# Channel-major tensors and row tiles by token residue modulo 16, with only the pooling input in time order

## The reference, cut to what matters

```
u     = rms_norm(x) * g                     # x: (4, 4096, 1024)
proj  = u @ w_in                            # 5120 columns: a, gate, p, two gates
v     = a * sigmoid(gate)                   # GLU
v     = depthwise_causal_conv(v, width 31)  # over time
v     = swish(layer_norm(v)) @ w_conv_out   # conv branch
z     = trailing_mean(p, w) - p             # w = 2, 4, 8, 16, one per group of 256 channels
z     = (z @ pool_w[g]) * pool_scale @ w_pool_out
h     = x + rms_norm((g_conv * v + g_pool * z) @ w_o)
out   = h + rms_norm(square(relu(rms_norm(h) @ w_ff1)) @ w_ff2)
```

## Time and profile before

| | us |
|---|---|
| time, median of 3 runs | 975.74 |
| time, lowest | 975.29 |
| time of the profiled execution | 976.0 |
| span of its slowest core (the spans run from 971.7 to 974.4) | 974.4 |
| busy in that span: PE / DVE / ACT / POOL | 949.2 / 451.3 / 277.6 / 62.6 |

### The profile page before, as it was taken

How to read it: one execution, slowest core, us unless ns; L and a number is a source line. 1 busy time by engine, 2 the same in 40 slices (tenths; PEclk the granted TensorE clock), 3 DMA queues, 4 the chain that set the end, 5 groups by cost and what they waited for, 6 DMA issues and landing times.

```text
span 974.4 us, 14114 instructions; the slowest of 8 cores (971.7 to 974.4 us)
## 1 busy us (share of the span) xinstructions
PE 949.2 (97%) x4971; PEld 484.2 (50%) x4971; DVE 451.3 (46%) x767; ACT 277.6 (28%) x531; POOL 62.6 (6%) x112
## 2 busy tenths in 40 slices
PE   7789999999999999999999999999999999999996
PEld 4655666665545544444444444444444444444444
DVE  4478886575482114566666630344223431244222
ACT  4553111132114431333335530233202330133211
POOL 1010001000010000121213200000000000000000
PEclk9999999999999999999999999999999999999999
DMA  9995165976780021759989995220022001210021
GB/s 183 253 146 74 17 89 105 143 109 115 118 140 1 1 87 15 143 117 191 168 190 178 196 197 90 87 87 1 1 87 87 1 1 44 87 43 1 1 86 66
DMA packets 93111, 91.21 MB, mean 94 GB/s; under 512 B 43601, under 2 KB 74577, under 8 KB 92914
## 3 DMA queue, kind: packets, MB, share of 16 engines
q0 software_dynamic: 32416, 35.13, 26.2%
q1 hardware_dynamic: 60626, 55.18, 21.1%
HBM read 98.88 MB, written 16.84 MB: 119 GB/s over the span
## 4 chain that ended last, share of the span: by engine, by line
PE 91%; DMA 3%; DVE 3%; ACT 1%; issue 1%; DVEq 0%; ACTq 0%; SPq 0%
PE ps L220 90%; DMA arena<-w_in 2%; DMA arena<-xh 1%; ACT arena L238 1%; PE ps L223 1%; DVE arena L246 1%; DVE arena L250 1%; DVE arena L477 0%; DMA arena<-arena 0%; DVE arena L241 0%; ACT sm L238 0%; DVE arena L256 0%; DVEq L159 0%; DVE sm L400 0%; ACTq L159 0%
## 5 line engine op out<-in xcount | busy, mean ns | idle before, releaser
L220 PE MATMUL ps<-arena 128*128 128x512 bf16 (+4 forms) x4731 | 937.9, 360 | 13.9 <-DVE arena L246 2.8
L220 PEld LDWEIGHTS ps<-arena 128*128 128x128 bf16 (+1 forms) x4731 | 470.1, 103 | 473.4 <-issue 25.7
L238 ACT ACTIVATE arena<-ps 128x512 bf16<-128x512 f32 (+5 forms) x346 | 203.0, 593 | 622.1 <-PE ps L220 467.0
L246 DVE TENSOR_SCALAR ps<-ps 128x512 f32<-128x512 f32 x128 | 89.1, 699 | 110.9 <-PE ps L220 110.2
L241 DVE TENSOR_TENSOR ps<-ps,arena 128x512 f32<-128x512 f32 (+1 forms) x65 | 43.6, 688 | 176.1 <-ACT arena L238 175.6
L250 DVE SCALAR_TENSOR_TENSOR arena<-arena,ps 128x512 bf16<-128x512 f32 (+1 forms) x64 | 43.9, 686 | 133.0 <-ACT arena L238 111.0
L241 DVE TENSOR_TENSOR arena<-ps,arena 128x512 bf16<-128x512 f32 (+2 forms) x52 | 42.3, 830 | 35.6 <-ACT arena L238 29.6
L238 ACT ACTIVATE arena<-arena 128x1024 bf16<-128x1024 f32 (+1 forms) x33 | 34.8, 1054 | 46.3 <-DVE arena L250 35.8
L250 DVE SCALAR_TENSOR_TENSOR arena<-ps,sm,arena 128x512 f32<-128x512 f32 (+1 forms) x65 | 45.1, 737 | 5.0 <-DVE sm L400 3.0
L250 DVE SCALAR_TENSOR_TENSOR arena<-arena,sm 128x1024 bf16<-128x1024 f32 (+1 forms) x33 | 42.3, 1282 | 4.3 <-POOL sm L396 2.4
L241 DVE TENSOR_TENSOR arena<-arena 128x512 bf16<-128x512 f32 (+2 forms) x56 | 38.4, 690 | 4.3
(11 more groups left out here) (34 smaller groups left out, 91.3 us busy)
## 6 DMA issues: line engine op xcount, KB each, us to landing
arena<-xh SPq DMA_DIRECT2D x32, 512.0 KB, 8.6
arena<-w_ff POOLq DMA_DIRECT2D x16, 1024.0 KB, 27.8
out<-arena SPq DMA_DIRECT2D x31, 512.0 KB, 3.1
arena<-out SPq DMA_DIRECT2D x16, 512.0 KB, 4.1
arena<-w_in POOLq DMA_DIRECT2D x12, 512.0 KB, 13.1
arena<-w_in POOLq DMA_DIRECT2D x2, 2048.0 KB, 17.2
arena<-gb SPq DMA_DIRECT2D x4, 512.0 KB, 6.4
arena<-w_pool_out POOLq DMA_DIRECT2D x2, 1024.0 KB, 23.1
```

The source lines that it names most:

```text
L220: kb.op("pe", lambda e: e.matmul(o, lhsT=l, rhs=r, start=start, stop=stop), [l, r], [o])
L238: kb.op("act", lambda e: e.activation(out=o, in_=i, func=func, **kw), rd, wr)
L246: kb.op("dve", lambda e: e.tensor_scalar(out=o, in0=a, scalar1=s1, scalar2=s2, op0=op0, **kw), rd, [o])
```

## The change

Columns of `uT`, `z`, `s_t` and all that follows them no longer run in time. Column r*128 + m now holds token 16*m + r. A tile j of x and of the output is the 128 rows j, j+16, j+32, ..., each still 4 KB long, 64 KB apart in DRAM. `p_t` stays in time order, so that the copies from PSUM write it in steps of 16 columns (64 bytes), with the 16 halo columns as a copy of their own, and every pooling task now writes `z` in steps of 128 columns (256 bytes). Since a residue tile spans all of time, a pooling task needs the whole row of its chunk: the tasks are queued only behind block 3 of a chunk. The `p_group`s go in the order 0, 7, 1, 2, 3, 6, 5, 4; one task is emitted behind each of the last eight, two behind each pair of `q` = 0 and one behind each of `q` = 1. The stationary operand of a GLU product becomes 128 neighbouring columns, and the activation of `cv_t3` writes them in one piece (its input view is left as it was).

```diff
--- before.py
+++ after.py
@@ -187,6 +187,8 @@
     gbd = din("gb", [5, DM])
     convw = din("convw", [8, 128, 16 * 3 * 16])
     out = nc.dram_tensor("out", [NT, DM], F32, kind="ExternalOutput").ap()
+    xrows = xh[H:TT, :].rearrange("(m r) d -> r m d", r=16)
+    orows = out.rearrange("(m r) d -> r m d", r=16)
     hud = nc.dram_tensor("hu_scratch", [H, DM], BF16, kind="Internal").ap()
 
     with ExitStack() as es:
@@ -358,8 +360,8 @@
         wev = []
 
         def x_load(j):
-            P, r0 = (32, 0) if j < 0 else (128, H + 128 * j)
-            xev[j] = LOAD(xst[x_buf[x_order.index(j)]][:P], xh[r0:r0 + P, :].rearrange("p (k t) -> p k t", k=8),
+            P, src = (32, xh[0:32, :]) if j < 0 else (128, xrows[j])
+            xev[j] = LOAD(xst[x_buf[x_order.index(j)]][:P], src.rearrange("p (k t) -> p k t", k=8),
                           after=[wev[j - 4]] if j in (4, 5, 6) else [])
 
         LOAD(grow, gbd[0:1, :])
@@ -454,14 +456,16 @@
             w = POOL_W[g]
             c0 = 32 + blk * 512
             pc = p_t[:, cc, :]
-            zo = z[:, cc, blk * 512:(blk + 1) * 512]
+            zo = z[:, cc, :].rearrange("p (r m) -> p m r", r=16)[:, 32 * blk:32 * (blk + 1), :]
+            z0 = z[:, cc, :].rearrange("p (r m) -> p m r", r=16)[:, 0, :]
+            tm = lambda v: v.rearrange("p (m r) -> p m r", r=16)
             if g == 0:
-                TTE("dve", zo, pc[:, c0 - 1:c0 + 511], pc[:, c0:c0 + 512], ALU.subtract)
+                TTE("dve", zo, tm(pc[:, c0 - 1:c0 + 511]), tm(pc[:, c0:c0 + 512]), ALU.subtract)
                 if blk == 0:
                     t1 = scr16
                     TTE("dve", t1, pc[:, 31:47], pc[:, 32:48], ALU.add)
                     TTE("dve", t1, t1, inv[:, 0, :], ALU.mult)
-                    STT(zo[:, 0:16], pc[:, 32:48], -2.0, t1, ALU.mult, ALU.add)
+                    STT(z0, pc[:, 32:48], -2.0, t1, ALU.mult, ALU.add)
                 return
             sb = s2b[2] if g == 1 else s2b[cc % 2]
             if g == 1:
@@ -479,11 +483,11 @@
                 if blk < 3:
                     COPY("dve", carry[:, cc:cc + 1], so[:, n - 1:n])
                 sl = so[:, n - 512:n]
-            STT(zo, sl, 1.0 / w, pc[:, c0:c0 + 512], ALU.mult, ALU.subtract)
+            STT(zo, tm(sl), 1.0 / w, tm(pc[:, c0:c0 + 512]), ALU.mult, ALU.subtract)
             if blk == 0:
                 t1 = scr16
                 TTE("dve", t1, sl[:, 0:16], inv[:, g, :], ALU.mult)
-                TTE("dve", zo[:, 0:16], t1, pc[:, 32:48], ALU.subtract)
+                TTE("dve", z0, t1, pc[:, 32:48], ALU.subtract)
 
         scr = T("scr", [128, 16 + 8], F32)
         scr16 = scr[:, 0:16]
@@ -495,7 +499,12 @@
             b = banks(1)
             for k in range(8):
                 MM(ps[:, b, 0:n], w_p[:, k, cc * 128:(cc + 1) * 128], uT[:, k, H + t0:H + t0 + n], k == 0, k == 7)
-            COPY(eng, p_t[:, cc, 32 + t0:32 + t0 + n], ps[:, b, 0:n])
+            h = max(-t0, 0)
+            if h:
+                COPY(eng, p_t[:, cc, 32 - h:32], ps[:, b, 0:h])
+            r0, r1 = (t0 + h) // 128, (t0 + n) // 128
+            COPY(eng, p_t[:, cc, 32:2080].rearrange("p (m r) -> p r m", r=16)[:, r0:r1, :],
+                 ps[:, b, h:n].rearrange("p (r m) -> p r m", m=128))
 
 
         def wg_load(q):
@@ -532,14 +541,13 @@
             (trn, 7), (pu, 6, 2), (nrm, 9), (pu, 7, 2), (pu, 0, 3), (nrm, 10), (pu, 1, 3), (pu, 2, 3), (nrm, 11),
             (pu, 3, 3), (pu, 4, 3), (nrm, 12), (pu, 5, 3), (nrm, 13), (pu, 6, 3), (nrm, 14), (wg_load, 0), (pu, 7, 3),
             (nrm, 15), (wg_load, 1)])
-        for blk in range(2):
-            for cc in range(8):
-                pq(cc, blk)
         for blk in range(2, 4):
-            for cc in range(8):
+            for cc in pools:
                 pg(cc, blk)
-                pq(cc, blk)
-                pool_pump(1)
+                if blk == 3:
+                    for b in range(4):
+                        pq(cc, b)
+                    pool_pump(1)
 
 
         def conv_load(cc):
@@ -576,7 +584,7 @@
             for i in range(2):
                 r = 2 * rp + i
                 for k in range(8):
-                    MM(ps[:, b + i, :], uT[:, k, H + r:H + NT:16], wg[q % 2][:, k, :, :].rearrange("p a n -> p (a n)"), k == 0, k == 7)
+                    MM(ps[:, b + i, :], uT[:, k, H + r * 128:H + (r + 1) * 128], wg[q % 2][:, k, :, :].rearrange("p a n -> p (a n)"), k == 0, k == 7)
             sg = sig[st["sig"]]
             st["sig"] ^= 1
             sg = sg.rearrange("p (a n) -> p a n", a=2)
@@ -659,7 +667,7 @@
                 glu_pair(q, rp)
                 if steps:
                     steps.popleft()()
-                pool_pump(1)
+                pool_pump(2 if q == 0 else 1)
                 pump(3)
                 if q == 3 and rp % 2 == 0:
                     weff_group(rp // 2)
@@ -709,7 +717,7 @@
             TS(v, v, bnag[:, r, 0:1], ALU.subtract, lnr[:, r:r + 1], ALU.mult)
 
         def cv_t3(cc):
-            sv = s_t[:, cc, :].rearrange("p (m r) -> p m r", r=16)
+            sv = s_t[:, cc, :].rearrange("p (r m) -> p r m", r=16)
             pbs = []
             for half in range(2):
                 b = banks(1)
@@ -718,7 +726,7 @@
                 for r8 in range(8):
                     TR(pb[:, r8 * 128:(r8 + 1) * 128], cv[:, cc, half * 8 + r8, :], identb[:])
             for half in range(2):
-                ACT(sv[:, :, half * 8:half * 8 + 8], pbs[half].rearrange("p (r m) -> p m r", r=8), AF.Silu,
+                ACT(sv[:, half * 8:half * 8 + 8, :], pbs[half].rearrange("p (r m) -> p r m", r=8), AF.Silu,
                     bias=vcol(8, cc), scale=vcol(0, cc))
 
         for blk in range(4):
@@ -752,7 +760,7 @@
         outh = {}
 
         def x_reload(j):
-            LOAD(xr[j % 3], xh[H + 128 * j:H + 128 * (j + 1), :])
+            LOAD(xr[j % 3], xrows[j])
 
         def resid_sq(p, c0, gb_t, junk, ac):
 
@@ -779,7 +787,7 @@
                     if c0 <= c < c0 + n:
                         rs = res[:, c:c + p.shape[1]]
                         STT(rs, p, r, rs, ALU.mult, ALU.add)
-                rs, dst = res[:, c0:c0 + n], out[128 * j:128 * (j + 1), c0:c0 + n]
+                rs, dst = res[:, c0:c0 + n], orows[j][:, c0:c0 + n]
                 outh[j, c0] = kb.op("sp", lambda e, rs=rs, dst=dst: e.dma_start(out=dst, in_=rs), [rs], [("outh", j)], dma=True)
 
         def halves(b):
@@ -865,7 +873,7 @@
 
         def ff2_end(b, j):
             res = xres[j % 2]
-            LOAD(res, out[128 * j:128 * (j + 1), :], reads=[("outh", j)])
+            LOAD(res, orows[j], reads=[("outh", j)])
             resid_b(halves(b), resid_a(b, gb3, 0, hT[j // 4][:, 0, :], "act"), res, j)
 
         def ff2_tile(j):
```

## The result

The changed kernel takes 1031.35 us where the kernel before takes 975.67: 1.06 times as long, 95% interval 1.0507 to 1.0694. The forecast was 985.5 with a range to 1000. Where executions of an experiment were disturbed (two of four of the one called e3, one of four of e2, one of eleven of e7), the others stand for it.

The account below looks back on a forecast made before the run. TensorE, busy 97% of the span, was taken to bound the kernel, with VectorE's queue on its path in the GLU stage. 7.5 + 1.6 + 0.7 = 9.8 us on 976.0, less 0.3, gave 985.5, range 977 to 1000.

Parts of the forecast that it names:

- Steps in writing: Stepped copies into p_t and pooling writes of z: between nothing and 0.53 us for 512 columns on VectorE, taken as nothing.
- The first rival: Stepped writes cost the full 0.53 us, VectorE falls further behind and ScalarE's ramp copies lengthen: 998 us; chance 0.22.
- the ramp: Before the GLU stage, eight more copies of 16 columns on ScalarE: 0.7 us, between 0 and 1.4.
- The moved pooling: Pooling moved from the ramp's end into GLU part 0 makes VectorE late with conv weights, delaying TensorE: 7.5 us.
- the clock: Behind TensorE's wait of some 6 us for conv weights, a lower granted clock costs 1.6 us, bounds 0 and 3.2.
- its wait: In GLU part 1, TensorE waits some 6 us for conv weights, ready at 141.4.
- The weight loads of the GLU: TensorE's loads for GLU products fall from 142 to 98 ns each, and give nothing.
- Loads of x with rows 64 KB apart: Loading tiles of x as 4 KB rows 64 KB apart: taken as 0, bounds 0 and 3 us.

Follow-up runs that it names:

- e3: The changed kernel, but the copies from PSUM write p_t contiguously; this also let the first three pooling tasks start early: 1023.6 and 1024.9 us.
- e2: The kernel before, all tensors in time order, with only the changed kernel's order of groups and pooling tasks: 986.62 us (1.0098).
- e7: The kernel before, with transposes and activations of the conv branch's last four chunks one step earlier in the gated stage: 974.6 us (0.9989).
- the rulers: Two kernels that compute no block and time single operations by write and read pattern: 512 lone bf16 every 256 bytes take 2436 ns, contiguous ones 690 ns.
- e1: The changed kernel, but each pooling task writes its 512 columns of z contiguously instead of in steps: 985.85 us (1.0088).
- e9: The changed kernel with p_t written contiguously, plus a memset making VectorE's first pooling task wait for chunk 0's whole row: 1030.68 us (1.0555).
- e8: The kernel before, but the pooling branch's gate product reads uT as TensorE's moving operand in steps of 16 columns (32 bytes): 1198.95 us (1.2286).
- e4: The kernel before in its own order, but every pooling task writes z in the changed kernel's steps: 1018.97 us (1.0429).

## Why the prediction was wrong

**The step that failed is "Steps in writing".** It bounded the cost of writing `z` between nothing and a doubling (0.53 us), and took nothing. Measured are 1.745 us in the operation and 1.65 from task to task (the next operation's delay in it). The row it leaned on, the conv eviction, steps in PSUM, in f32, and in reading; `z` is SBUF, bf16, and written. All three differ, and the rulers size it. SBUF instead of PSUM costs a third of a microsecond: 512 columns in steps take 692 ns from PSUM (every 32 bytes), in SBUF 1014 to 1016 where they are read and 1023 where f32 is written. That the elements have two bytes and are written costs the other 1.4: 2436. The upper end was no bound at all, because no row stood behind a doubling.

A rule that the prediction quoted bears on it: the Trainium skill ("Advanced Engine Details and Errata", section "SBUF Cachelines") wants two hits in a 16-byte line. For f32 and for reading the rulers agree (f32 written every 8 bytes 693, every 16 bytes 1064; read 692 and 1062). For lone bf16 they don't: every 8 bytes a line has two hits, and it is 1296.

**The first rival had the right mechanism and its rate.** It put 2.4 us on the end for each 0.1 us of the step. With 1.745, that is 42 us on 985.5, or 1027, and the time came out at 1031.35 (e1 puts 45.5 us on the step, 2.6 for each 0.1). The rival's 1.7 us more for longer copies in the ramp doesn't show: e9 has 0.7 for all of them. The price was wrong, and with it the range's upper end.

**The rest of the sum held in the main.** The moved pooling was forecast at 7.5 us, the clock at 1.6, the ramp at 0.7, together 9.8; e1 measures 985.85 for just these, and its wait comes 1.5 us from its place. In e2 the first two are 10.3. The ramp's term was too large: TensorE starts the groups of block 2 at 58.50 instead of 58.16, and at 58.53 in e9, which has the copies in runs. Missed was the 1.24 us that the new order of the conv branch gives back, counted at nothing: in the order of residues a gated block of 512 columns needs one of a chunk's two activations, not both (e7). So it is partly luck that e1 comes within 0.4 us of the forecast: the first two terms are 10.3 instead of 9.1, and the missed gain goes the other way.

**What was said of TensorE held.** The weight loads of the GLU fall to 102 ns (9.69 us by 95 between 88 and 117; forecast 98), and give nothing: in e1, where TensorE isn't held up yet, the sigmoids of two pairs start at 104.86 and 108.31, 3.45 us apart as before. Loads of x with rows 64 KB apart land in 8.9 us on the median instead of 8.6; the one on the chain that ended last takes 12.83, where it took 13.54.

Open: what in the writing of half a word costs 4.45 ns a line was not taken further than the two rulers.

## What to carry to other kernels

A new order of columns must be paid where some engine steps: choose VectorE's reading (0.36 us for 512 columns here) or its writing of whole words, not TensorE's moving operand (e8), and let the writes of 2-byte data be runs that fill 4-byte words. Before an operation is called cheap by a row, check that the row has the same memory, the same width and the same direction; if none has, the upper bound is open, and a kernel that times only that operation closes it in one run. A price on an engine that is half idle on the mean is paid nearly in full where that engine's queue is the path: in e4 42.6 of some 53 us, in a stage that took a tenth of the span.

## What the runs showed of the hardware

- Written every 16 bytes or more, a lone bf16 column costs 4.45 ns, a lone f32 column 1.68, in a VectorE operation with two inputs (a copy of bf16 to lone bf16 takes 1277 ns for 512); ScalarE takes 2390 ns for 512 lone bf16 too, where a run takes 597. Aligned pairs of bf16 are free at 64 bytes (693 against 690), and the same pairs one column on are not (1273).
- A GLU product behind such a write starts 0.38 us before the write's recorded end (126.72, where 124.67 and 2.43 make 127.10) and takes 0.2 us longer, 0.89 instead of 0.69.
- VectorE reads PSUM every 32 bytes at full pace (692), SBUF every 64 bytes at 1014.
- With its moving operand in steps of 32 bytes a product of 512 columns takes TensorE 0.92 us, at a granted clock of 1.00 as at 0.50, where a contiguous one takes 0.216 and 0.43. In e8 the clock falls to 0.50 within each group of eight such products in three places of its trace (near 270, 280 and 304), though TensorE is busy without a gap.
